# Folds and their vectors ahead of the row roots, three conditioning pieces moved, and a part of the first norm on GpSimd

## Time and profile before

| | us |
|---|---|
| median of 3 runs | 2371.89 (2370.17 to 2371.92) |
| the profiled execution's own time | 2370.85 |
| its span | 2369.0 |
| TensorE busy | 2326.4 |
| VectorE busy | 1895.6 |
| ScalarE busy | 1138.0 |
| GpSimd busy | 5.7 |

### The profile page before, as it was taken

One profiled execution on the slowest core, in us unless ns is written; L12 is line 12 of the kernel. 1 busy time (PEld: TensorE's weight loads), 2 busy tenths in 40 slices (PEclk: granted clock), 3 DMA queues, 4 the chain that ended last, 5 costly groups with the idle time before them and its releaser, 6 DMA issues.

```text
span 2369.0 us, 32294 instructions
## 1 busy us (share of the span) xinstructions
PE 2326.4 (98%) x13232; PEld 2025.4 (85%) x13232; DVE 1895.6 (80%) x2144; ACT 1138.0 (48%) x1431; POOL 5.7 (0%) x11
## 2 busy tenths in 40 slices
PE   5899999999999999999999999999999999999999
PEld 3588888889888888888889888898888888989987
DVE  6888898899888778889768787887887666886754
ACT  2253445547555334555446444644555334665552
POOL 0000000000000000000000000000000000000000
PEclk9899999999999999999999999999999999999999
DMA  9989777785777788878765788866777774674343
GB/s 396 364 332 351 277 290 274 246 297 178 278 279 271 249 272 292 290 280 289 247 209 191 280 320 317 289 241 243 281 279 272 279 273 168 226 274 150 125 168 135
DMA packets 119011, 620.23 MB, mean 262 GB/s; under 512 B 13392, under 2 KB 14672, under 8 KB 76112
## 3 DMA queue, kind: packets, MB, share of 16 engines
q1 hardware_dynamic: 70560, 446.40, 53.3%
q10 hardware_dynamic: 48304, 171.76, 19.5%
HBM read 616.01 MB, written 2.10 MB: 261 GB/s over the span
## 4 chain that ended last, share of the span: by engine, by line
PE 93%; DVE 4%; DMA 2%; issue 0%; ACT 0%; SPq 0%; DVEq 0%; ACTq 0%
PE pm L647 25%; PE pm L648 13%; PE ps L647 13%; PE ps L648 6%; PE pm L705 5%; PE pm L706 5%; PE pm L707 5%; PE ps L705 2%; PE ps L706 2%; PE ps L707 2%; DVE acc_first L1848 2%; PE pm L662 1%; PE pm L661 1%; PE pm L663 1%; DMA e<-in_ada 1%; DMA ada<-in_ada 1%
## 5 line engine op out<-in xcount | busy, mean ns | idle before, releaser
L1782 DVE TENSOR_TENSOR w_lo<-raw,w_hi 128x2048 fp32r<-128x2048 f32 (+2 forms) x412 | 892.1, 2166 | 329.3 <-ACT w_hi L1219 328.0
L1219 ACT ACTIVATE w_hi<-raw 128x2048 fp32r<-128x2048 f32 (+2 forms) x412 | 747.6, 1815 | 545.3 <-DMA raw<-in_w_down 112.1
L647 PE MATMUL pm<-h,w_hi 128*128 128x512 f32 x1534 | 529.7, 391 | 1.5 <-DVE w_lo L1782 0.7
L648 PE MATMUL pm<-h,w_lo 128*128 128x256 f32 x1534 | 424.4, 277 | 0.0
L1794 DVE SCALAR_TENSOR_TENSOR acc<-ada,csil,acc 128x1024 f32<-128x1024 f32 x300 | 384.0, 1280 | 1.5
L647 PEld LDWEIGHTS pm<-h,w_hi 128*128 128x128 f32 x1534 | 288.0, 188 | 63.6 <-issue 3.2
L648 PEld LDWEIGHTS pm<-h,w_lo 128*128 128x128 f32 x1534 | 288.0, 188 | 0.2
L647 PE MATMUL ps<-h,w_hi 128*128 128x512 f32 x786 | 271.8, 391 | 0.0
L648 PE MATMUL ps<-h,w_lo 128*128 128x256 f32 x786 | 217.4, 277 | 0.0
L647 PE MATMUL pm<-h_sgu,w_hi 128*128 128x512 f32 x608 | 209.1, 391 | 0.0
L647 PEld LDWEIGHTS ps<-h,w_hi 128*128 128x128 f32 x786 | 147.6, 188 | 31.4 <-issue 0.7
(11 more groups left out here) (512 smaller groups left out, 4088.4 us busy)
## 6 DMA issues: line engine op xcount, KB each, us to landing
ada<-in_ada ACTq DMA_DIRECT2D x320, 512.0 KB, 5.7
raw<-in_w_up SPq DMA_DIRECT2D x88, 1024.0 KB, 5.0
raw<-in_w_in SPq DMA_DIRECT2D x56, 1024.0 KB, 5.5
raw<-in_w_down SPq DMA_DIRECT2D x64, 704.0 KB, 4.8
raw<-in_sgu_u SPq DMA_DIRECT2D x32, 1024.0 KB, 5.4
raw<-in_sgu_v SPq DMA_DIRECT2D x32, 1024.0 KB, 5.2
raw<-in_sgu_z SPq DMA_DIRECT2D x32, 1024.0 KB, 4.9
raw<-in_sgu_out SPq DMA_DIRECT2D x32, 1024.0 KB, 4.9
```

Of the source, the lines that this page charges most:

```text
L647: pe.matmul(dst[:, :], wh[:, k, :], hl, start=(kc == 0), stop=False, skip_group_check=True)
L648: mm = pe.matmul(dst[:, 0:T], wl[:, k, :], hi, start=False, stop=last, skip_group_check=True)
L1219: act.activation(hi_(q, n), raw_(q, n), ACT.Copy).then_inc(hi_ready, 1)
L1782: tt_(lo_(q, n), raw_(q, n), whole(hi_(q, n)), ALU.subtract).then_inc(lo_ready, 1)
```

## The change

Five edits, made together:

- GpSimd gets the split of weight piece 2 (`q = len(FIRST_LOADS) - 1`) and the low halves of chunks 4 to 7, each as an addition of the shift in place and a subtraction, with the semaphore `xn_shifted` between them. VectorE loses both: `FIRST_SPLITS` has two entries, and `first_low(1)` is left out.
- VectorE waits at the end of the first stage for `lo_ready` of three pieces.
- `ADA_SPANS`: 21 instead of 24 conditioning pieces in the 15 slots from vb 0, 15 instead of 12 in the 9 slots from w_out 0.
- `fold_group(5)` goes behind piece 30 of 32 of sgu_out and `fold_group(6)` behind piece 13 of 16 of mla_out (counted from 0), in place of the ends of these products.
- `take_group(5)`, `post_gain(0)` and `modulation("pre1")` go ahead of `row_roots` in sgu_out, `take_group(6)` and `post_gain(1)` in mla_out.

```diff
-FIRST_SPLITS = [(1, 11), (2, 1), (2, 10)]
+FIRST_SPLITS = [(1, 11), (2, 1)]
-... ("vb", 0, 15, 24), ("w_out", 0, 9, 12),
+... ("vb", 0, 15, 21), ("w_out", 0, 9, 15),
 # TensorE
-                tokens("sgu_out", blk, (...) if blk == 0 else None, src=y_part)
-            fold_group(5)
+                tokens("sgu_out", blk, (...) if blk == 0 else None,
+                       lambda j: fold_group(5) if j == NPIECES["sgu_out"] - 2 else None, src=y_part)
-                tokens("mla_out", blk, last_heads if blk == 0 else None)
-            fold_group(6)
+                tokens("mla_out", blk, last_heads if blk == 0 else None,
+                       lambda j: fold_group(6) if j == NPIECES["mla_out"] - 3 else None)
 # GpSimd
+            q = len(FIRST_LOADS) - 1
+            pool.wait_ge(lo_ready, q)
+            pool.wait_ge(hi_ready, q + 1)
+            n = elems(q)
+            pool.tensor_tensor(lo_(q, n), raw_(q, n), whole(hi_(q, n)), ALU.subtract).then_inc(lo_ready, 1)
+            for kc in range(4, 8):
+                pool.wait_ge(hh_ready, kc + 1)
+                pool.tensor_scalar(nt[:, kc % 4, :], nt[:, kc % 4, :], mod(SH1, kc), None, ALU.add).then_inc(xn_shifted, 1)
+                pool.wait_ge(xn_shifted, kc - 3)
+                pool.tensor_tensor(h[:, kc, T:2 * T], nt[:, kc % 4, :], whole(h[:, kc, 0:T]), ALU.subtract).then_inc(h_ready, 1)
 # VectorE
-                    if q and k == 7:
+                    if q and q != 2 and k == 7:
                         first_low(q - 1)
...
             first_low(QUARTERS - 1)
+            dve.wait_ge(lo_ready, len(FIRST_LOADS))
...
+            take_group(5)
             post_gain(0, G0)
+            modulation("pre1", "pre", KC, C1)
             row_roots("sgu_out", y0_tok, diag0, 0)
-            take_group(5)
-            modulation("pre1", "pre", KC, C1)
...
-            row_roots("mla_out", y_tok, diag, 8)
             take_group(6)
             post_gain(1, G1)
+            row_roots("mla_out", y_tok, diag, 8)
```

More of the change, by code:

```diff
@@ L105 @@
 N_DVE = [sum(len(K_DVE[i]) for i in range(q)) for q in range(QUARTERS + 1)]
-FIRST_SPLITS = [(1, 11), (2, 1), (2, 10)]
+FIRST_SPLITS = [(1, 11), (2, 1)]
 FIRST_USED = N_DVE[QUARTERS]
-ADA_SPANS = [("ka", 4, 12, 18), ("va", 0, 8, 14), ("qb", 0, 16, 28), ("vb", 0, 15, 24), ("w_out", 0, 9, 12),
+ADA_SPANS = [("ka", 4, 12, 18), ("va", 0, 8, 14), ("qb", 0, 16, 28), ("vb", 0, 15, 21), ("w_out", 0, 9, 15),
              ("w_up0", 6, 37, 32), ("w_down0", 0, 32, 18), ("w_up1", 0, 44, 42), ("w_down1", 0, 12, 4), ("sgu_v", 0, 32, 40),
@@ L373, in build @@
         xn_ready = sem("xn_ready")
+        xn_shifted = sem("xn_shifted")
         hh_ready = sem("hh_ready")
@@ L1014, in _ @@
             for blk in range(TOKENS["sgu_out"]):
-                tokens("sgu_out", blk, (lambda kc: pe.wait_ge(y_lo_ready, kc + 1)) if blk == 0 else None, src=y_part)
-            fold_group(5)
+                tokens("sgu_out", blk, (lambda kc: pe.wait_ge(y_lo_ready, kc + 1)) if blk == 0 else None,
+                       lambda j: fold_group(5) if j == NPIECES["sgu_out"] - 2 else None, src=y_part)
             def scaled_turn(bank_, y_, dg, kc, tt):
```

## The result

The changed kernel took 2386.83 us (median of 6 runs, 2383.06 to 2393.89) against 2372.26 us for the kernel before in the same runs (6, 2370.17 to 2379.49): ratio 1.0059, 95% interval 1.0043 to 1.0076. The profiled execution took 2390.57 us, its span is 2388.8 us.

The account below looks back on a forecast made before the run. TensorE was taken to bound the kernel, in the first stage through last sums waiting for VectorE. 11.3 + 0.4 + 0.1 - 0.7 = +11.1 us on the median 2371.89 gave 2383.0 us, range 2370 to 2387.

Parts of the forecast that it names:

- the slack: First stage: the gates may end up to 80.9 us at no cost; after that each us costs the kernel one.
- the gates' end: First stage, last matmuls of gate_part(1), which need GpSimd's low halves: forecast at 92.0 us, 11.1 past the allowed 80.9.
- rival (3): As forecast, but TensorE falls to half clock again before the first stage's last sums: +14.2 us, 2386; chance 0.11.
- part 1: First stage, GpSimd's share of the norm (one split, four low halves): late gates +11.1 us, clock net +0.2, together +11.3.
- part 2: Conditioning moved from vb/oa to w_out: ends -1.6 us, w_out and the wait of fold_group(1) +2.2, net +0.4.
- Taking turns: First stage: GpSimd and VectorE exclude each other; the split holds VectorE 3.84 us, the eight small instructions 3.32.
- the 4.1 of my sum: First stage: the 2048-wide split on GpSimd was taken to last 4.1 us.
- Queues and clock: First stage: loads stall at no further cost; half clock at 92 us +3.3, none at the last sums -3.1.
- Part 3: Folds and vectors moved ahead of the row roots: sgu_out +0.1 us, mla_out -0.7.

Follow-up runs that it names:

- quiet: pool_only with VectorE stopped behind its piece (2, 7) until GpSimd's four low halves are done; ratio 1.0037 to the kernel before.
- folds_only: The kernel before with only the two folds and their vectors moved ahead of the row roots in sgu_out and mla_out; ratio 0.9993.
- rest_only: The change without GpSimd's share: conditioning moved to w_out, both folds and their vectors ahead of the row roots; ratio 1.0011 to the kernel before.
- rest_late: rest_only with the fold of group 1 behind column 10 of w_out in place of 9; 2370.96 us, ratio 0.9982 to the kernel before.
- the probe: The kernel before plus seven GpSimd instructions on the input at the start, for which the fourth piece's load waits; its own time tells nothing.
- best: The kernel before with three conditioning packets moved from vb to w_out, group 1's fold one column later, mla_out's fold and vectors earlier; 2369.39 us, ratio 0.9985.
- lows_only: The kernel before with only the low halves of the second quarter moved to GpSimd, the split left on VectorE; ratio 1.0031.
- pool_only: The kernel before with GpSimd's share alone, the third split and the second quarter's low halves; 2383.77 us, ratio 1.0047.

## Why the prediction was right, and where a term was off

**The place and the slack: right.** The stage's end hangs on the gates' end; "the gates may end up to 80.9 us at no cost" puts the mark 36.9 us behind the gates, four kernels have 36.1 to 36.3. The gates' end was forecast at 92.0 and is 92.31; forecast +11.3, measured +10.7.

**How near the number is, and by what luck.** The forecast was 2383.0 us and the median is 2386.83, which is nearer to the 2386 of rival (3). But that rival's sign, half clock at the last sums, is absent in the profiled execution. Two errors inside part 1 cancelled, part 2 was a microsecond too low, and the profiled execution of the changed kernel holds 8.3 us that no part forecast.

**Taking turns: right, but two terms were wrong and made up for each other.** The split lasts 4.76 us, not 4.1, and GpSimd reaches the first addition 0.5 us late. It blocks VectorE for 3.93 us (6.60 against the 2.67 that such a pair takes), where I had 3.84. The small instructions I had right in number and in kind, each behind one VectorE piece. But I let each hold VectorE for 0.35 to 0.48 us, 3.32 in all; measured are 0.58 + 0.21 + 0.28 = 1.07 us from 81.28 on. What made up for it is at the end and in between. VectorE finishes its pieces at 89.85 us, and GpSimd still has 1.59 us to go where I had 0.3: its last addition ends 0.79 us behind VectorE's last piece, and the subtraction comes after that. The gaps of 0.10 us between VectorE's pieces were left out too. The pace came out right: four pairs in 12.8 us, where I had 13.0. The Trainium skill's page SBUF — State Buffer, section Who interferes with whom, calls the sharing an exclusive lock. The trace agrees for the 2048-wide instructions on either engine (4.27 us lost in 4.58; 2.95 us for an addition beside VectorE's split); for the small ones only GpSimd's side shows it in full. The page writes "fully blocks" of VectorE's 2-port modes and of instructions with two SBUF inputs only that they contend; the prediction read the two together, and the 3.93 us of hold on such a pair bear it out here. The Trainium skill's GPSIMD Engine Reference, section 3.1 Elementwise, has 4497 ns for a 2048-wide tensor_tensor. The trace agrees: quiet shows 4.49 us, so the 4.1 of my sum was too low.

**Queues and clock: right in kind.** "The DMA share drops for a while": 0.01 from 85 to 90, 0.00 from 90 to 95 and 0.43 from 95 to 100, forecast from 84 to 97. VectorE's take, forecast at 104, came at 101.88. Half clock came with the long wait (0.50 from 80 to 90 us), not only at 92, and the last sums took 1.05 us, at full clock, as forecast. What I took for a fixed cost of the kernel before is not fixed: in folds_only, rest_only, rest_late and the probe TensorE ran at full clock from 100 to 115 us, with no wait ahead of the last sums, and the mark is 116.1 to 116.6. They had their half clock earlier: from 85 to 90 us the granted clock is 0.50 in all four, where the kernel before has 1.00. TensorE came later to the last sums for it, and the wait did not arise. The profiled execution of before, and best, waited there (3.30 and 2.08 us), fell to half clock and have 117.8. So the loss of the stage is 10.7 to 12.4 us, by which execution it is held against. With the 1.25 us of parts 2 and 3 below that makes 12.0 to 13.7 us; the medians are 14.6 us apart and the two fastest runs 12.9.

**Part 2: forecast +0.4, measured +1.4.** "TensorE's wait of 1.62 us at 442.56 goes: -1.6" gave -2.0. "fold_group(1) waits 2.0" gave 1.88, but the clock behind it was left out. TensorE in the changed kernel:

```profile
527.46 0.46 PE L627 MATMUL pv<-fold,sel 128*128 128x128 f32 x2 [1.88 <-DVE fold L1810]
...
528.62 0.63 PE L648 MATMUL pm<-h,w_hi 128*128 128x512 f32 x1
...
531.75 0.39 PE L648 MATMUL pm<-h,w_hi 128*128 128x512 f32 x1
```

Five pairs of matmuls are 0.64 us apart there and not 0.34: 1.5 us, together 3.4. The same price fell due in rest_only and was absent in rest_late and best. The wait of 1.62 us in the kernel before had brought no such fall: the clock column is 1.00 from 440 to 446 us.

**Part 3: forecast -0.6, measured -0.15.** In sgu_out root and square stand as forecast; ScalarE in the changed kernel:

```profile
2011.17 0.20 ACT L1653 ACTIVATE stat<-stat 128x1 f32<-128x1 f32 x1 [2.09 <-DVE stat L2340]
2011.28 0.58 ACT L1649 ACTIVATE sq_out<-pm 128x512 f32<-128x512 f32 x1
```

The root now comes ahead of the square, gain and loss cancel, +0.25 for my +0.1. In mla_out (VectorE, changed kernel, beside the earlier trace rows)

```profile
2374.45 0.16 DVE L2339 TENSOR_REDUCE stat<-stat 128x1 f32<-128x4 f32 x1 [8.12 <-ACT sq_out L1649]
...
2379.01 6.36 DVE L2353 SCALAR_TENSOR_TENSOR x<-px,gain,x 128x256 f32<-128x256 f32 x16 [0.20 <-PE px L1022]
```

the first pair follows the reduce by 4.56 us where it was 5.29: -0.73. The fold inside the stream costs 0.3, not 0.2, so -0.4. At the end of the span even that is hardly seen: in folds_only the last pair ends 0.84 us earlier than before and the kernel 0.3.

**What no part of mine explains.** Of the 19.8 us between the two spans, 11.5 are there at 899 us and 8.3 come by 1195. TensorE is busy there for 295.0 of 296 us, and 295.3 before, at a granted clock of 1.00, with fewer matmuls in the time (1693 against 1738). TensorE from 950 to 1150 us in the changed kernel, and then in folds_only:

```profile
L648 PE MATMUL pm<-h,w_hi 128*128 128x512 f32 x383 | 134.6, 395 | 0.0
```

```profile
L647 PE MATMUL pm<-h,w_hi 128*128 128x512 f32 x390 | 133.2, 389 | 0.0
```

rest_only gained 7.4 us of delay over the same stretch, rest_late 7.6, quiet 7.1, lows_only 6.9, pool_only, folds_only and best changed by 0.4 or less. It is not bound to an edit, and the runs of the kernel before reach from 2367.49 to 2384.03 us. In the changed kernel the slower matmuls begin at 926.53 us, behind TensorE's wait of 0.98 us for VectorE, and last until 1180; the kernel before waited 0.72 us at the same place and kept 389 ns. In rest_only they begin without a wait. Where it comes from was not tried.

## What to carry to other kernels

Work that goes from VectorE to GpSimd is not off VectorE's hands: beside VectorE instructions with two SBUF inputs, as nearly all were here, a wide GpSimd instruction stops VectorE for nearly its whole length, and a narrow one costs GpSimd the rest of whatever VectorE is in. The only VectorE instruction with one input that ran beside GpSimd in the changed kernel took 0.96 us for 0.75, by a narrow one; a wide one beside it was not tried. Give GpSimd what nobody asks for soon, and put first on it what the in-order reader wants first: the order of the same two jobs was worth 8.1 us of the first stage. And price a new wait of TensorE with the clock behind it, here 1.5 us on top of 1.9.

## What the runs showed of the hardware

- A GpSimd addition of a scalar to 128x256 takes 0.93 us and a subtraction 0.72 with VectorE idle; mostly 1.89 and 1.12 against VectorE pieces of 1.28 us (up to 2.23 and 1.64), and 2.95 for an addition against a VectorE split. The scalar from memory or as a constant made little difference (0.92 and 0.85 us at least).
- The block is lopsided: eight narrow GpSimd instructions cost VectorE 1.07 us, one wide one 3.9 to 4.3.
- With the same instructions and a clock column of 1.00, TensorE's wide matmuls take 389 ns in some stretches and 395 in others, worth 2.1 us in w_out and 7 to 8 from 899 to 1195 us. Both occur in one execution: the kernel before has 389 at 440 us and 395 from 444 to 450. The longest stretch of 395 lasts about 290 us (rest_late, from 875).
- A wait of 1.88 us of TensorE in the middle of a busy stream was followed by about 3 us at half clock in the changed kernel and in rest_only, one of 1.62 us (before) was not.
